# A transform split by token parity in an fp32 two-block network on one core

## The reference

```
def bidir_long_conv(u, h, skip):        # u (1, 256, 512)
    k = concat([h[:, 0], zeros, h[:0:-1, 1]])
    U = rfft(u, n=512); Kf = rfft(k, n=512)
    return irfft(U * Kf)[:, :256] + u * skip
z = parts[0]
for o in range(2):
    z = parts[o + 1] * bidir_long_conv(z, filt[:, o], skip[o])
```

## Time and profile before

| | us |
|---|---|
| median of 3 runs | 2279.82 (2279.41 to 2280.49) |
| span of the profiled execution | 2277.7 |
| PE busy | 1903.6 (84%) |
| DVE busy | 1029.9 (45%) |
| ACT busy | 652.3 (29%) |
| DMA, mean over the span | 290 GB/s of 659.76 MB |

### The profile page before, as it was taken

How to read it: one execution, slowest core, us unless ns; L and a number is a source line. 1 busy time by engine, 2 the same in 40 slices (tenths; PEclk the granted TensorE clock), 3 DMA queues, 4 the chain that set the end, 5 groups by cost and what they waited for, 6 DMA issues and landing times.

```text
span 2277.7 us, 26862 instructions
## 1 busy us (share of the span) xinstructions
PE 1903.6 (84%) x11468; PEld 1313.5 (58%) x11468; DVE 1029.9 (45%) x1337; ACT 652.3 (29%) x737; POOL 9.3 (0%) x6
## 2 busy tenths in 40 slices
PE   7999997655656666565676999999999999999998
PEld 3988782111111111111122888898888888898887
DVE  6777572000000000000012767567767767567766
ACT  4444240000000000000002434564434434564333
POOL 1000000000000000000000000000000000000000
PEclk9999998888888778878888999999999999999999
DMA  9361689999999999999999555435445555434442
GB/s 385 139 263 75 261 357 415 431 432 432 433 432 432 431 431 431 432 431 432 433 432 424 199 196 196 174 142 194 185 185 191 209 196 194 176 131 185 185 185 102
DMA packets 36253, 659.76 MB, mean 290 GB/s; under 512 B 4024, under 2 KB 4536, under 8 KB 6976
## 3 DMA queue, kind: packets, MB, share of 16 engines
q1 hardware_dynamic: 34144, 650.56, 69.4%
q10 hardware_dynamic: 2016, 7.84, 0.9%
HBM read 657.34 MB, written 1.05 MB: 289 GB/s over the span
## 4 chain that ended last, share of the span: by engine, by line
PE 61%; DMA 32%; DVE 5%; ACT 2%; issue 1%; SPq 0%; ACTq 0%; DVEq 0%
PE ps L1652 59%; DMA ring_b<-experts_dram 20%; DMA ring<-experts_dram 9%; DMA ring<-stream_dram 2%; PE ps L1661 1%; DVE area_n L1434 0%; ACT area_n L790 0%; DVE ring_lo L1056 0%; DVE expert_area L1374 0%; DVE x_tok L1445 0%; DVE tail L1165 0%; DVE tail L1172 0%; ACT x_r L565 0%; ACT u_both L797 0%; DVE area_h L1351 0%
## 5 line engine op out<-in xcount | busy, mean ns | idle before, releaser
L1387 DVE TENSOR_TENSOR ring_lo<-ring,w_hi 128x2048 fp32r<-128x2048 f32 x168 | 384.7, 2291 | 196.2 <-ACT w_hi L749 196.2
L1652 PE MATMUL ps<-u_both,w_hi 128*128 128x512 f32 (+1 forms) x1792 | 413.5, 362 | 0.0
L749 ACT CAST w_hi<-ring 128x2048 fp32r<-128x2048 f32 x168 | 320.9, 1910 | 246.6 <-PE ps L1652 209.8
L1652 PEld LDWEIGHTS ps<-u_both,w_hi 128*128 128x128 f32 x1792 | 312.8, 190 | 44.1 <-issue 0.7
L1652 PE MATMUL ps<-u_both,ring_lo 128*128 128x256 f32 x1536 | 251.1, 283 | 0.0
L725 ACT ACTIVATE expert_area<-ps 128x512 f32<-128x512 f32 x16 | 9.6, 597 | 834.3 <-PE ps L1652 834.3
L1652 PEld LDWEIGHTS ps<-u_both,ring_lo 128*128 128x128 f32 x1536 | 223.8, 191 | 12.4
L1652 PE MATMUL ps<-ring_b,area_h 128*32 128x512 f32 x976 | 147.3, 758 | 95.7 <-DMA ring_b<-experts_dram 87.3
L1358 DVE TENSOR_TENSOR expert_area<-expert_area,ps 128x512 f32<-128x512 f32 x16 | 11.0, 688 | 460.6 <-PE ps L1652 460.6
L1652 PE MATMUL ps<-ring,area_h 128*32 128x512 f32 x1024 | 146.2, 725 | 85.3 <-DMA ring<-experts_dram 77.5
L1652 PEld LDWEIGHTS ps<-ring_b,area_h 128*32 128x32 f32 x976 | 34.9, 135 | 202.5 <-DMA ring_b<-experts_dram 107.7
(11 more groups left out here) (404 smaller groups left out, 2312.0 us busy)
## 6 DMA issues: line engine op xcount, KB each, us to landing
ring<-stream_dram SPq DMA_DIRECT2D x114, 2048.0 KB, 7.5
ring_b<-experts_dram SPq DMA_DIRECT2D x45, 4096.0 KB, 31.1
ring<-experts_dram SPq DMA_DIRECT2D x45, 4096.0 KB, 31.0
ring<-experts_dram SPq DMA_DIRECT2D x5, 2048.0 KB, 16.7
ring_b<-experts_dram SPq DMA_DIRECT2D x6, 1024.0 KB, 9.4
area_n<-norm_rows_dram ACTq DMA_DIRECT2D x6, 512.0 KB, 6.0
x_tok<-x_dram SPq DMA_DIRECT2D x2, 1024.0 KB, 7.9
spare<-experts_dram SPq DMA_DIRECT2D x1, 2048.0 KB, 19.1
```

Source lines behind the costliest of these rows:

```text
L749: A.copy(upper_part(n), ring[:, n % RING, :]).then_inc(sig("alone_hi_ready") if n in ALONE else sig("w_hi_ready"), 1)
L1387: V.tensor_tensor(ring_lo[:, n % RING, :], ring[:, n % RING, :], upper_part(n).bitcast(F32), ALU.subtract).then_inc(sig("alone_ready") if ...
L1652: ins = M.matmul(out, lhsT, rhs, start=start, stop=stop, **more)
```

## The change

The forward transform uses that bins k and 255-k have the same cosines and sines up to the sign of the odd tokens. Even and odd tokens are transformed apart with 128 columns of table each (four matmuls of 128x512 in place of eight), and DVE adds and subtracts the two halves; ACT copies the odd half to SBUF first. The way back is split in the same way: DVE forms sum and difference of the two halves of the bins, and PE makes even and odd tokens apart (sixteen matmuls of 128x128 in place of 128x256). Transposes read z with a step of two tokens, and the skip step reads and writes z with a step of two. The tables shrink, one spectrum term changes its sign. The merge-gate units get other banks and other places in PE's order: 32 goes before the `hm` transposes, 35 and the first half of 36 before the first inverse transform, 37 around the second forward transform; `ada(7, range(0, 2), 2)`, the user of slots 36 and 37, goes from before to after the second forward transform. On DVE, `lower_first(21)` (slot 42) goes from the end of order 0 into the middle of order 1.

```diff
@@ -75,13 +75,13 @@
-LAST_BANKS = (6, 4, 5, 6, 4)
+LATE_BANKS = (5, 2, 3, 6, 7, 6, 4, 5, 6)
-    return 2 + n % 2 if n < 32 else 5 if n == 32 else 6 + n % 2 if n < 36 else LAST_BANKS[n - 36]
+    return 2 + n % 2 if n < 32 else LATE_BANKS[n - 32]
@@ -112,7 +112,7 @@
-TABS, N_TABS = offsets(("dft", 2 * TT * T), ("idft", 2 * TT * T), ("causal", 2 * 384))
+TABS, N_TABS = offsets(("dft", 2 * 2 * P), ("idft", 2 * 2 * P), ("causal", 2 * 384))
@@ -258,8 +258,8 @@
-        dft = r.take(2, TT, T)
-        idft = r.take(2, TT, T)
+        dft = r.take(2, 2, P)
+        idft = r.take(2, 2, P)
@@ -282,6 +282,7 @@
+        odd_z = tail[:, raw_at + 2048:raw_at + 2048 + 2 * HYC].rearrange("p (j c) -> p j c", j=2)
@@ -660,19 +661,21 @@
                 if o >= 1:
-                    act.wait_ge(sig("signal_ps"), ORDERS + o)
+                    act.wait_ge(sig("signal_ps"), ORDERS + 2 * o)
                 A.copy(z_tok, ps[:, 4:6, :]).then_inc(sig("z_kept"), 1)
...
                     merge_gates(31, of=ACT.Identity)
+                act.wait_ge(sig("signal_ps"), ORDERS + 2 * o + 1)
+                A.copy(odd_z, ps[:, 2:4, :]).then_inc(sig("hT_odd"), 1)
+                if o == 0:
                     act.wait_ge(sig("hsum_ready"), 1)
...
                     upper_first(20)
-                    merge_gates(34, 35)
+                    merge_gates(34, 35, 36)
                 else:
-                    merge_gates(36)
                     upper_first(21)
@@ -993,7 +996,7 @@
-                V.tensor_tensor(spec[:, o, 1, 1, :], odd[:, 1, :], n, ALU.subtract).then_inc(sig("spec_kept"), 1)
+                V.tensor_tensor(spec[:, o, 1, 1, :], n, odd[:, 1, :], ALU.subtract).then_inc(sig("spec_kept"), 1)
@@ -1197,6 +1200,14 @@
                             ALU.mult).then_inc(sig("hm_ready"), 1)
+            def signal_halves(o, i):
+
+                dve.wait_ge(sig("hT_odd"), ORDERS + o + 1)
+                dve.wait_ge(sig("signal_ps"), ORDERS + 2 * o + 2)
+                V.tensor_tensor(yspec[:, i, 0, :], bank(i), odd_z[:, i, :], ALU.add)
+                return V.tensor_tensor(yspec[:, i, 1, :], bank(i), odd_z[:, i, :], ALU.subtract)
+
+            signal_halves(0, 0)
             dve.wait_ge(sig("hmT_ps"), 1)
@@ -1205,17 +1216,22 @@
             for o in range(ORDERS):
-                dve.wait_ge(sig("signal_ps"), ORDERS + o + 1)
+                if o == 1:
+                    signal_halves(o, 0)
+                step(signal_halves(o, 1))
                 for t in range(TT):
-                    re, im = bank(t), bank(2 + t)
+                    re, im = yspec[:, 0, t, :], yspec[:, 1, t, :]
                     V.tensor_tensor(yt[:, 0, :], re, spec[:, o, 0, t, :], ALU.mult)
...
                     V.tensor_tensor(yspec[:, 0, t, :], yt[:, 0, :], yt[:, 1, :], ALU.subtract)
-                    last = V.tensor_tensor(yspec[:, 1, t, :], yt[:, 2, :], yt[:, 3, :], ALU.add)
-                    if t == 0:
-                        step(last)
+                    step(V.tensor_tensor(yspec[:, 1, t, :], yt[:, 2, :], yt[:, 3, :], ALU.add))
+                    if o == 1 and t == 0:
+                        lower_first(21)
+                for i in range(2):
+                    V.tensor_tensor(yt[:, 2 * i, :], yspec[:, i, 0, :], yspec[:, i, 1, :], ALU.add)
+                    last = V.tensor_tensor(yt[:, 2 * i + 1, :], yspec[:, i, 0, :], yspec[:, i, 1, :], ALU.subtract)
                 last.then_inc(sig("yspec_ready"), 1)
@@ -1229,12 +1245,11 @@
                     z = hy(4 * o + j)
-                    step(V.scalar_tensor_tensor(z, z, col("skip", 4 * o + j),
-                                                bank(4 + j // 2)[:, (j % 2) * T:(j % 2 + 1) * T], ALU.mult, ALU.add))
+                    by_parity = z.rearrange("p (m e) -> p e m", e=2)
+                    y = bank(4 + j // 2)[:, (j % 2) * T:(j % 2 + 1) * T].rearrange("p (e m) -> p e m", e=2)
+                    step(V.scalar_tensor_tensor(by_parity, by_parity, col("skip", 4 * o + j), y, ALU.mult, ALU.add))
                     last = V.tensor_tensor(hy(4 * o + 4 + j), hy(4 * o + 4 + j), z, ALU.mult)
                 last.then_inc(sig("z_done"), 1)
-                if o == 0:
-                    lower_first(21)
 
@@ -1865,11 +1880,13 @@
                 for n, k0, k1 in steps:
-                    if k0 == 0 and (n < 32 or 34 <= n <= 36):
+                    if k0 == 0 and n < 32:
 
                         pe.wait_ge(sig("unit_kept"), max(n - 1, 25))
-                    elif n >= 39:
-                        pe.wait_ge(sig("unit_kept"), n - 2)
+                    elif k0 == 0 and n == 37:
+                        pe.wait_ge(sig("unit_kept"), 36)
+                    elif n == 40:
+                        pe.wait_ge(sig("unit_kept"), 38)
                     unit(bank(merge_bank(n)), 14 + (n - 25) // 2, (n - 25) % 2, k0, k1)
@@ -1908,40 +1925,41 @@
                 if o == 1:
-                    merge_steps((36, 0, 4))
+                    merge_steps((36, 4, KD))
                     pe.wait_ge(sig("z_done"), 1)
...
                     for j in range(4):
-                        turn(bank(4 + t)[:, j * P:(j + 1) * P], hy(4 * o + j)[:, t * P:(t + 1) * P],
+                        turn(bank(4 + t)[:, j * P:(j + 1) * P], hy(4 * o + j)[:, t::2],
                              ready=sig("z_ps") if t == 1 and j == 3 else None)
...
                 else:
-                    merge_steps((36, 4, KD))
-                    pe.wait_ge(sig("unit_kept"), 36)
-                    ada(7, range(0, 2), 2)
+                    merge_steps((37, 0, 4))
                 pe.wait_ge(sig("z_kept"), o + 1)
...
                     pe.wait_ge(sig("inter_kept"), 2 * H)
-                for j in range(2):
-                    for k in range(TT):
-                        for t in range(TT):
-                            mm(bank(2 * j + k), dft[:, j, t, k * P:(k + 1) * P], z_tok[:, t, :],
-                               start=t == 0, stop=t == 1,
-                               ready=sig("signal_ps") if j == k == t == 1 else None)
+                for e in (1, 0):
+                    for j in range(2):
+                        mm(bank(2 * e + j), dft[:, j, e, :], z_tok[:, e, :], ready=sig("signal_ps") if j == 1 else None)
                 if o == 0:
 
+                    merge_units(32)
                     pe.wait_ge(sig("hm_ready"), 1)
...
                                  ready=sig("hmT_ps") if h == 3 and t == 1 else None)
-                    merge_units(32)
+                    pe.wait_ge(sig("hT_odd"), ORDERS + 1)
+                    merge_units(33, 34)
                     pe.wait_ge(sig("hm_ready"), 2)
-                    merge_units(33, 34)
+                    merge_steps((35, 0, KD), (36, 0, 4))
+                    pe.wait_ge(sig("unit_kept"), 33)
                 else:
-                    merge_units(37, 38)
+                    merge_steps((37, 4, KD))
+                    pe.wait_ge(sig("unit_kept"), 37)
+                    ada(7, range(0, 2), 2)
+                    merge_units(38)
                     ada(7, range(2, 5), 2)
@@ -1949,15 +1967,11 @@
                 for j in range(4):
-                    n = 0
-                    for i in range(2):
-                        for k in range(TT):
-                            mm(bank(4 + j // 2)[:, (j % 2) * T:(j % 2 + 1) * T], yspec[:, i, k, j * P:(j + 1) * P],
-                               idft[:, i, k, :], start=n == 0, stop=n == 3,
-                               ready=sig("conv_ps") if j == n == 3 else None)
-                            n += 1
-                if o == 0:
-                    merge_units(35)
+                    for e in range(2):
+                        for i in range(2):
+                            at = (j % 2) * T + e * P
+                            mm(bank(4 + j // 2)[:, at:at + P], yt[:, 2 * i + e, j * P:(j + 1) * P], idft[:, i, e, :],
+                               start=i == 0, stop=i == 1, ready=sig("conv_ps") if j == 3 and e == i == 1 else None)
 
@@ -2423,13 +2437,12 @@
     half_t = half.transpose(2, 0, 1, 3).reshape(P, -1).astype(f)
-    dft_t = dft.reshape(2, TT, P, T).transpose(2, 0, 1, 3).reshape(P, -1)
-    idft_t = (dft.transpose(0, 2, 1) / T).reshape(2, TT, P, T).transpose(2, 0, 1, 3).reshape(P, -1)
+    idft_t = (dft[:, :, 0:P] / T).reshape(2, P, 2, P).transpose(3, 0, 2, 1).reshape(P, -1)
     s, q = np.arange(P)[:, None], np.arange(P)[None, :]
...
     causal = np.concatenate([big, fwd, zero, zero, bwd, big], axis=1)
-    tabs = np.concatenate([dft_t, idft_t, causal], axis=1).astype(f)
+    tabs = np.concatenate([half_t, idft_t, causal], axis=1).astype(f)
     const = np.concatenate([np.eye(P), np.ones((P, P)), np.tile(t, (P, 1))], axis=1).astype(f)
...
     tl = np.linspace(0.0, 1.0, T, dtype=f)[:, None]
```

## The result

Ten runs of each kernel, side by side: 2286.61 us (median, 2282.66 to 2288.01) after, 2279.74 (2279.40 to 2281.99) before. The ratio is 1.0025, 95% interval 1.0017 to 1.0033: 0.25% slower. The profiled execution after took 2286.58 us with a span of 2284.8, so it is a typical one; it stands against the span of 2277.7 in the earlier trace rows.

A forecast was written before the change was run, and what follows sets the result against it. PE's timeline up to `branch(0, 0)` was taken to bound the kernel, the shift reaching the end. 13.6 us less PE work, offset by late slots, waits and clock, left 1.7 us: 2279.82 + 1.7 = 2281.5, range 2278 to 2286.5.

The forecast's parts named there:

- VectorE's chain: Order 0, before the first inverse: added operations make yspec_ready 237.8 instead of 233.8 us, and PE idles 2.9 us.
- landing of pair 42/43: Transfer ahead of unit 39: takes 7.4 us once issued and lands at 263.6 us, against 261.0 before.
- within 0.2%: Whole kernel: the time changes by no more than 0.2%, 4.6 us, either way; chance 0.73.
- Transforms: PE, per order: forward transform 3.6 us instead of 7.11, inverse 3.9 instead of 7.17; 13.6 us less work for both orders.
- Rival (c): Both inverses: not shortened, 7.2 us in place of 3.9, giving 2287.6 us; chance 0.05.
- the step that takes the gain: Order 1: late ada steps delay issue of pair 42/43 by 6.6 us; PE idles 6 us before unit 39.
- Step of two: Skip steps and transposes touching z: nothing extra; if each access doubled, 1.9 us and 1.0 more.
- rival (b): Transposes and skip steps: the step of two halves the rate, 4.5 us over the forecast, 2286; chance 0.13.
- Clock in the short gaps: PE's gaps before the first inverse and second transposes: 0.8 us lost together, between none and 3.4.
- half clock behind the long hole: Units 39 and 40, after PE idles 6 us: half clock expected, costing 1.7 us.
- Pair 48/49 and `branch(0, 0)`: End of the stage: the pair lands at 286.6 us; PE, ready at 290.3, starts the branch at 290.8, 1.7 later.
- One for one to the end: From the first branch, near 289 us, to the end: PE's gain or loss carries through in full.

The follow-up runs named there:

- e1: The changed kernel run again with nothing altered, four runs: 2286.9 us, ratio 1.0043.
- e11: The changed kernel without VectorE's eight added sums of order 0, left out and not done elsewhere: 2279.61 us, ratio 0.9998.
- e9: The changed kernel with gate units and ada steps dealt as in the kernel before, so the new transforms alone: 2284.53 us, ratio 1.0021.
- e3: The changed kernel with three, two and seven unread fp32 products put in PE's three holes: 2279.5 us, ratio 1.0003.
- e4: The kernel before with only the two ada steps moved late, behind the second forward transform and unit 37: 2287.14 us, ratio 1.0036.
- e5: The changed kernel with two ada steps ahead of the second transposes and unit 36's second half ahead of the first inverse: 2273.61 us, ratio 0.9977.
- e6: e5 with three unread fp32 products added ahead of unit 39: 2275.14 us, ratio 0.9979.
- e10: e9 with four unread fp32 products added ahead of the first inverse: 2283.80 us, ratio 1.0023.
- e2: The changed kernel with the two ada steps put back ahead of the second transposes: 2276.76 us, ratio 0.9993.
- e7: The changed kernel with the routing stage filled by unread products and a stream product moved between the two logit groups: 2284.24 us, ratio 1.0023.
- e8: The changed kernel with the alterations of e6 and e7 together: 2274.53 us, ratio 0.9977.

## Why the prediction was right, and where it was off

The prediction forecast 2281.5 us in a range to 2286.5, and the median lies at 2286.6, 0.1 above the range. The sign is right, and so is the mechanism up to the router: VectorE's chain, the three holes and what ended each. The size is not: +1.7 us forecast, +6.9 measured. Up to the router the profile has +4.7 (e1 +3.1), since the clock in the first gap was taken 0.8 to 2.1 us too small and the landing of pair 42/43 by 1.3; the rest comes behind the router. Its calling the change "within 0.2%" is off, since the loss is 0.25% (0.17 to 0.33).

**Transforms.** Forecast 3.6 and 3.9 us, measured 3.67 and 3.84. The floor of 0.118 us per record holds, 3.84 / 32 = 0.120; e11 has the shortest, 3.73. Rival (c) is refuted. By the 107 ns that the Trainium skill (TensorE: Matmul & The Clock Gate, LDWEIGHTS) gives for a weight load the inverse would be 3.4 us, as an estimate, which no profile shows.

**VectorE's chain.** Forecast 21.35 us from forward transform to inverse (237.8 - 216.45), measured 21.31. e11 confirms it by taking the sums away. The prediction had this term in full and then made too little of it: it called pair 42/43, released late by the new deal, "the step that takes the gain", while e9 shows 5 of the 7 us with the old deal too. The pair is the last link in e9 as well (a wait of 5.32 us), but there VectorE's chain and the clock make it late.

**Step of two.** Forecast nothing extra. The skip steps take 0.48 us, as in the earlier trace rows. PE's eight transposes take 1.12 us for the first order instead of 1.04, so their step of two costs 0.08 us, not 1.0; rival (b) is refuted. So is the mechanism that was to carry the upper part of the range: the time came out at 2286 for another reason, and that the range reaches so far is luck. The Trainium skill (SBUF — State Buffer, Door 1: The DMA port swizzle) has a stride of up to four fp32 free; the skip steps' 0.48 us agree.

**Clock in the short gaps.** Forecast 0.8 us for both. Measured: the first inverse 6.74 us in the profile, 5.44 in e1, against 3.84 with the gap filled (e3). That is 2.9 or 1.6 for the one gap of 3.23 us, within the prediction's end of 3.4. This term was mis-sized; the drop of 1.4 to 1.7 that the expert stage showed was not an upper end for one gap. Behind the second gap (2.17 us) nothing was lost in either profile: the forward transform took 3.60 us. The half clock behind the long hole was sized rightly, 1.7 forecast against 7.7 - 5.9 = 1.8 us for units 39 and 40.

**Landing of pair 42/43.** Forecast 7.4 us, measured 264.44 - 255.73 = 8.7; why it took longer is open. Together with the clock, unit 39 starts 54.1 us behind the forward transform where the forecast had 51.6; the wait is 7.36 us where it had 6. In e1, with the milder drop, it is 52.9.

**Pair 48/49 and `branch(0, 0)`.** `branch(0, 0)` starts 291.52 - 214.65 = 76.9 us behind the forward transform, forecast 74.4, before 72.7. PE waits 0.47 us for this pair, as forecast (0.5). Unit 39 to the router's transposes is only 0.5 us shorter than before although the second inverse's 3.3 us of work are gone: 1.8 go into the half clock of units 39 and 40, 0.5 into this wait, and another 0.5 is lost behind it.

**"One for one to the end".** This step failed for the profiled run, which is one of the signs of being wrong that the prediction named. Behind the router's transposes it needs 1949.2 us, 4.2 more than before: 2.0 of them are the logits (4.8 us from the transposes to the first reduction of the logits before, 6.7 after), where PE's 32 narrow products took 5.77 us and ran partly at half clock. Another 2.1 come between the first and the second expert's results (VectorE's operations on them start 56.8 us apart, before 54.7, e1 54.3). The half clock in the router is not special to this kernel: the 32 products take 4.7 to 5.3 us in e3, e4, e5, e6, e9, e10 and e11, and 3.6 in e1 and e2. In the other profiles the stretch takes 1944.9 to 1947.2, among them e1 of the same kernel with 1945.1. So the shift does reach the end, and on top comes a loss behind the router that some runs have and others don't. What decides it, and how much of the median's 6.9 us it makes, stays open: e7 moved the median by 2.5 without settling it. With the measured shift up to the router the forecast's own sum would give 2279.8 + 4.7 = 2284.5 (2282.9 with e1's 3.1); for the 2 to 4 us from there to the median this loss is the candidate, not shown.

## What to carry to other kernels

Before work is moved from one engine to another, look at which of the two is later at that very place: PE made 61% of the chain and had hardly any idle time, but at the inverse it already waited 0.69 us for VectorE, so the sums given to VectorE there lengthened the path by 3.9 us; only the first two of the eight fell into a wait of its own. Reckon with a PE hole of 3 us twice, once for itself and once for the slower clock that may come behind it (1.6 and 2.9 us here), and deal movable work so that it fills the holes and frees the slots of the next transfer, in that order: here the same transforms gave 2286.6 or 2273.6 us, depending on where two ada steps and half a unit stood.

## What the runs showed of the hardware beyond what was expected

The same 32 products took 6.74, 6.17, 5.44 and 3.84 us. Behind a hole of 3.23 us every first inverse was slowed (after 6.74, e1 and e7 5.44, e2 5.34); behind 1.79 us it was at full clock in e5 and e6 (3.81) and at 5.44 in e8, so a hole of this length does it at times. The length alone does not decide: units 39 and 40 ran at full clock behind 2.96 us in e2 (5.9 us, granted 1.00) and partly at half clock behind 1.82 us in e5 (7.4 us, granted 0.50 from 260 to 263 us); the second forward transform took 3.60 us in the changed kernel and in e1, 4.16 in e7 and 4.44 in e11, each time behind a hole of 2.2 us. Filling holes with products that nobody reads brought 7 us in e3.

A change in one stage can make a kernel's time less steady: the kernel before spreads over 4.2 us in thirty-three runs, the changed one over 5.4 in ten and 10.4 in four. With such a spread one profile is no measure: e1's profile alone would have made the change 2.6 us slower, the medians say 7.
